# Per-head signals in the first block's attention, with the memory transposes and first scores moved into the last value chunk and the first memory-key chunk into the last steps

## The chip, the cores and the metric

The kernel runs on one core of one Trainium2 chip, in one launch. The metric is the device time of that launch in microseconds (us). The five engines of the core run their own instruction lists and meet only at semaphores: TensorE (PE in the rows, with PEld for its weight loads), VectorE (DVE), ScalarE (ACT), GpSimd (POOL) and SyncE (SP), which issues the weight loads.

## The reference, cut to what matters

Two transformer blocks on one sequence of 512 tokens, width 1024, all in float32.

- Block 1: RMS norm; a projection into eight heads of "forgetting" attention (head width 64, causal, each logit with a decay c_t - c_s from a cumulative sum of log gates) and eight heads of chunked attention with a relative bias; each head group normed; an output projection; residual. Then cross attention to 256 memory rows (four heads of width 256; the memory has its own RMS norm and a key/value projection `w_mem_kv`), residual; then SwiGLU of hidden width 2816, residual.
- Block 2: RMS norm; a projection of 4608 columns for three groups of dilated-window attention, whose queries and keys are normed per head; output projection, residual; RMS norm and a SwiGLU with a depthwise convolution of three taps; residual.

## The kernel before, in words

**Matmuls.** Float32 products are made from three matmuls on split operands (high part by high part, high by low, low by high; helper `three`, lines 1797 to 1799). Activations lie transposed in `a_hi` and `a_lo` (eight tiles of 128 features by 512 tokens). Weights come as chunks of 128 x 2048 (1 MB): SP loads a chunk into one of two `raw` slots, ACT copies it to `w_hi` (line 800), DVE, or POOL for some chunks (`pool_splits`), subtracts to get `w_lo` (line 1233, POOL 727), PE uses it. A slot is written again when the chunk that used it is done (`tile_done`), so the split of chunk c+1 runs beside PE's chunk c. All loops over chunks are in the order of the list `GEMMS`: forget, fox_qk, fox_v, chunk_qk, chunk_v, mem_k, mem_v, mix_out, mem_q, and so on. Each engine's order is written out by hand; nothing is planned by a tool.

**Around the attention of block 1.** PE ends `chunk_v` (two chunks of 48 matmuls; the second has four blocks b of 128 tokens, 12 matmuls each). Then it transposes the normed memory rows (16 transposes of 128 x 128, `turn`, line 2022, banks 4 to 7; ACT writes `a_hi`, line 1017, DVE `a_lo`, line 1551), then makes the scores of pairs 0 and 1 of heads, and begins the steps.

**The steps.** 32 pairs of heads (`HeadPair`): two heads by one block of 128 queries, i = b % 4 saying how many key blocks there are (i + 1). Pairs 0 to 15 have decays, pairs 16 to 31 a bias. At step t:

- PE: transposes of the probabilities of pair t (`pair_turned`, line 2161); scores of pair t + 2 (`pair_scores`, lines 2143, 2147, 2150); values of pair t (`pair_values`, through `by_column_group`, line 2048).
- DVE: `pair_out(t-1)` (line 1579), the reciprocal of the row sums and the copy of head 0's transposes to SBUF (`first_out`, lines 1588, 1591), the maxima of pair t + 2 (line 1563 with decays, 1570 with bias, where the biased scores are also written to `work`).
- ACT: the copy of head 1's transposes (`second_out`, line 1040), the two exponentials of pair t + 2 (`pair_exps`, lines 1029 and 1032).

One semaphore increment stands for both heads of a pair: `max_done`, `probs_done`, `turned`. The values of head 0 go to bank 2 and those of head 1 to bank 3, for every pair; so the values of pair t wait for `heads_done` of pair t - 1. After the last pair PE waits for all `heads_done` and begins `mem_k`: four chunks, each of two tiles of 24 matmuls with 256 columns.

**Three more places that the change touches.** (a) At `fox_qk` DVE works off the chain of the forget gates (lines 1491 to 1507), with the split of chunk 2 inside it, and only then evicts the tiles of chunk 0 (line 1520), whose banks chunk 2 of `fox_qk` writes. (b) Before `dil_in`: `residual` scales and adds eight tiles of the residual (POOL adds tiles 2 to 7, line 722) and writes `a_lo` (line 1281); `invert_pre("mixer_2")` then sums the eight squares in one reduction (line 1260); PE turns the sums to token order (`by_token`, line 1985), `invert_mixer` makes a diagonal (line 1271) and PE spreads it (`spread`, line 2014). (c) After `dil_out`: DVE adds its eight tiles to the residual (line 1741) and PE's `conv_up` waits (`enter`) until all eight are out of their banks; ACT splits the second chunk of `conv_up` before it makes `a_hi` of tiles 4 to 7, POOL subtracts for it (line 727), DVE writes `a_lo` (line 1281) and then sums the squares (line 1260).

## Time and profile before

| | |
|---|---|
| median of 3 runs | 1558.02 us (1558.0 to 1559.74) |
| the profiled execution's own time | 1563.09 us |
| its span in the profile | 1561.3 us |
| mean granted TensorE clock | 0.991 |
| PE busy | 1515.5 us, 97% of the span |
| PEld, DVE, ACT, POOL busy | 1235.7, 850.1, 602.0, 240.3 us |

The span is what the profile covers; the time of the execution lies 1.8 us above it. A busy time is the union of an engine's instructions; the ends of matmuls are modelled, so a PE shown busy may still be a PE at half clock, and the clock has its own column (1.00 is 2.4 GHz, 0.50 is 1.2 GHz). What PE waited for is in the view of waits; where in time, in the view by stretches and in the timeline.

### The profile page before, as it was taken

The page shows a single profiled execution, that of the slowest core. Times are in us where ns is not written, and L with a number is a line of the kernel's source. Part 1 is how long each engine was busy: PE and PEld are TensorE (multiplying, and loading weights), DVE is VectorE, ACT ScalarE, POOL GpSimd, SP SyncE. Part 2 cuts the span into 40 slices and gives each one's busy share as a digit, 9 for nine tenths or more (in the row PEclk, how much of TensorE's full clock was granted, in tenths as well). Part 3 has the DMA queues.
Part 4 walks back from the last instruction along what each step waited for, and adds up shares of the span by engine and source line. Part 5 has one row for each costly group of instructions (what it writes and reads, how often), then busy time and mean ns, then how long its engine had stood idle before and what let it go on. Part 6 is the DMA issues. An engine that isn't in the chain of part 4 may idle for free.

```text
span 1561.3 us, 21409 instructions
## 1 busy us (share of the span) xinstructions
PE 1515.5 (97%) x7988; PEld 1235.7 (79%) x7988; DVE 850.1 (54%) x1104; ACT 602.0 (39%) x923; POOL 240.3 (15%) x266
## 2 busy tenths in 40 slices
PE   9999988999998999999999899999999999999998
PEld 6787667887887888888888588888887788888887
DVE  6433564527545543433323786756876776767323
ACT  6222554643244322222323543335764433333222
POOL 0200000024014100000000554554542000000000
PEclk9999899999999999999999999999999999999999
DMA  5532002431112223333232123222002333232321
GB/s 166 190 97 92 1 2 64 153 108 54 55 55 81 81 81 107 93 96 108 81 107 90 50 77 108 81 98 91 2 1 82 96 91 107 81 107 82 109 105 54
DMA packets 152809, 132.22 MB, mean 85 GB/s; under 512 B 6300, under 2 KB 137628, under 8 KB 152740
## 3 DMA queue, kind: packets, MB, share of 16 engines
q1 hardware_dynamic: 150836, 128.11, 26.5%
q0 software_dynamic: 848, 3.17, 0.6%
q8 instruction: 46, 0.75, 0.2%
q14 instruction: 23, 0.19, 0.0%
q10 hardware_dynamic: 1056, 0.00, 0.0%
HBM read 129.15 MB, written 2.12 MB: 84 GB/s over the span
## 4 chain that ended last, share of the span: by engine, by line
PE 85%; DVE 5%; POOL 3%; ACT 3%; issue 3%; DMA 0%; ACTq 0%; SPq 0%; DVEq 0%; POOLq 0%
PE ps L1797 25%; PE ps L1798 25%; PE ps L1799 25%; PE ps L2048 2%; POOL other_stats L774 2%; PE ps L2161 1%; POOL x_t L722 1%; PE ps L2143 1%; PE ps L459 1%; PE ps L2058 1%; DVE a_lo L1281 1%; PE ps L1985 1%; ACT work L914 1%; PE ps L2014 0%; ACT w_hi L800 0%
## 5 line engine op out<-in xcount | busy, mean ns | idle before, releaser
L1797 PE MATMUL ps<-a_hi,w_hi 128*128 128x512 f32 (+2 forms) x1656 | 645.4, 390 | 14.8 <-DVE a_lo L1281 5.7
L1799 PE MATMUL ps<-a_hi,w_lo 128*128 128x512 f32 (+2 forms) x1656 | 639.9, 386 | 0.0
L1798 PE MATMUL ps<-a_lo,w_hi 128*128 128x512 f32 (+2 forms) x1656 | 639.8, 386 | 0.0
L1797 PEld LDWEIGHTS ps<-a_hi,w_hi 128*128 128x128 f32 (+1 forms) x1656 | 311.3, 188 | 87.9 <-issue 10.2
L1799 PEld LDWEIGHTS ps<-a_hi,w_lo 128*128 128x128 f32 (+1 forms) x1656 | 311.5, 188 | 64.0
L1798 PEld LDWEIGHTS ps<-a_lo,w_hi 128*128 128x128 f32 (+1 forms) x1656 | 311.6, 188 | 62.1 <-issue 0.7
L800 ACT ACTIVATE w_hi<-raw 128x2048 fp32r<-128x2048 f32 x118 | 225.8, 1913 | 348.5 <-PE ps L1799 346.4
L1233 DVE TENSOR_TENSOR w_lo<-raw,w_hi 128x2048 fp32r<-128x2048 f32 x94 | 215.3, 2290 | 245.0 <-ACT w_hi L800 244.7
L727 POOL TENSOR_TENSOR w_lo<-raw,w_hi 128x2048 fp32r<-128x2048 f32 x24 | 110.6, 4609 | 452.9 <-ACT w_hi L800 452.9
L1654 DVE TENSOR_TENSOR arena<-ps,rstd 128x512 f32<-128x512 f32 x88 | 60.2, 689 | 166.3 <-PE ps L1799 159.9
L1724 DVE RECIPROCAL rstd<-std 128x512 f32<-128x512 f32 x24 | 80.5, 3353 | 26.3 <-ACT std L1147 26.3
L1210 ACT ACTIVATE arena<-arena,vec 128x512 f32<-128x512 f32 x44 | 35.5, 815 | 110.3 <-DVE arena L1654 110.3
L1797 PE MATMUL ps<-w_hi,a_hi 128*128 128x512 f32 x192 | 74.9, 390 | 0.1
L1799 PE MATMUL ps<-w_hi,a_lo 128*128 128x512 f32 x192 | 74.9, 390 | 0.0
L1798 PE MATMUL ps<-w_lo,a_hi 128*128 128x512 f32 x192 | 74.9, 390 | 0.0
L2048 PEld LDWEIGHTS ps<-arena,work 128*64 128x64 f32 x1120 | 38.7, 138 | 27.2 <-issue 16.7
L2048 PE MATMUL ps<-arena,work 128*64 128x64 f32 x1120 | 47.1, 228 | 12.3 <-DVE work L1591 4.3
L1087 ACT ACTIVATE arena<-arena 128x512 f32<-128x512 f32 x22 | 13.9, 632 | 89.4 <-DVE arena L1654 89.4
L1775 DVE SCALAR_TENSOR_TENSOR arena<-arena,vec 128x384 f32<-128x384 f32 x88 | 48.0, 546 | 0.0
L1772 DVE SCALAR_TENSOR_TENSOR arena<-arena,vec 128x127 f32<-128x127 f32 x88 | 36.6, 416 | 12.6 <-DVE arena L1654 5.6
L1797 PEld LDWEIGHTS ps<-w_hi,a_hi 128*128 128x128 f32 x192 | 36.0, 188 | 8.1 <-DVE w_lo L1233 0.5
L1799 PEld LDWEIGHTS ps<-w_hi,a_lo 128*128 128x128 f32 x192 | 36.0, 188 | 7.6
(242 smaller groups left out, 1459.3 us busy)
## 6 DMA issues: line engine op xcount, KB each, us to landing
raw<-in_w_gate_up SPq DMA_DIRECT2D x44, 512.0 KB, 4.6
raw<-in_ffn_w_up SPq DMA_DIRECT2D x44, 512.0 KB, 4.6
raw<-in_attn_w_in SPq DMA_DIRECT2D x36, 512.0 KB, 4.4
raw<-in_w_in SPq DMA_DIRECT2D x24, 512.0 KB, 4.7
raw<-in_w_down SPq DMA_DIRECT2D x22, 512.0 KB, 4.0
raw<-in_ffn_w_down SPq DMA_DIRECT2D x22, 512.0 KB, 4.0
raw<-in_w_mem_kv SPq DMA_DIRECT2D x16, 512.0 KB, 4.2
raw<-in_w_out SPq DMA_DIRECT2D x8, 512.0 KB, 3.9
```

The lines of the kernel that those rows point to most:

```text
L727: pool.tensor_tensor(w_lo[:, ch.next_slot, :], raw[:, ch.next_slot, :], w_hi[:, ch.next_slot, :].bitcast(F), ALU.subtract).then_inc(weight ...
L800: act.activation(w_hi[:, ch.next_slot, :], raw[:, ch.next_slot, :], ACT.Copy).then_inc(weights_hi, 1)
L1210: act.activation(conv[:, 2 * ch.slot_o + j, :], up[:, 2 * ch.slot_o + j, :], ACT.Identity, bias=vcol("conv_b", ch.c + j * FT), scale=vcol( ...
L1233: dve.tensor_tensor(w_lo[:, ch.next_slot, :], raw[:, ch.next_slot, :], w_hi[:, ch.next_slot, :].bitcast(F), ALU.subtract).then_inc(weights ...
L1654: dve.tensor_tensor(up[:, 2 * ch.slot_o + j, :], ps[:, 2 * ch.slot_o + j, :], rstd[:, :], ALU.mult).then_inc(signal, 1)
L1724: dve.reciprocal(rstd[:, :], std[:, :]).then_inc(dil_rstd, 1)
L1772: dve.scalar_tensor_tensor(out=residues(u)[:, 0:tap, 1:128], in0=residues(src)[:, 4 - tap:4, 0:127], scalar=scalar, in1=residues(u)[:, 0:t ...
L1775: dve.scalar_tensor_tensor(out=u[:, tap * 128:S], in0=src[:, 0:S - tap * 128], scalar=scalar, in1=u[:, tap * 128:S], op0=ALU.mult, op1=ALU ...
L1797: pe.matmul(dst, s_hi, m_hi, start=start, stop=False, skip_group_check=across)
L1798: pe.matmul(dst, s_hi, m_lo, start=False, stop=False, skip_group_check=across)
L1799: return pe.matmul(dst, s_lo, m_hi, start=False, stop=stop, skip_group_check=across)
L2048: last = pe.matmul(dst[c, :], stationary[:, c], moving, start=start, stop=stop, skip_group_check=True)
```

## The change

1. **Signals by head.** New semaphores `pair_max`, `pair_probs` and `second_turned`: maxima, exponentials and transposes of a pair signal head by head, and what waits for them waits by head. With decays the one reduction over both heads becomes two. ACT's order at a step is: exponential of pair t + 1, head 0; copy of head 1's transposes of pair t; exponential of pair t + 1, head 1. DVE's is: maxima of t + 1, `pair_out(t-1)`, copy of head 0's transposes, reciprocal. The values of a pair lie in one bank (2 + b % 2), and wait for `heads_done` of pair t - 2.
2. **Inside the last value chunk.** PE's second `chunk_v` chunk has the 16 memory transposes after its block 0, the scores of pairs 0 and 1 after its block 2, then block 3. ACT's and DVE's lists are reordered to match, and ACT loads the table of the exponential earlier.
3. **First key chunk.** The two tiles of the first `mem_k` chunk take the place of the missing scores at steps 30 and 31 (banks 4 and 5); the second chunk writes banks 6 and 7, and only then PE waits for all `heads_done`. POOL makes both halves of the split of the second `mem_k` chunk during the attention.
4. **fox_qk.** The tiles of chunk 0 are evicted ahead of DVE's split of chunk 2.
5. **mixer_2.** Four squares are reduced, POOL adds tiles 4+5 and 6+7 in place, and DVE adds the two sums; the spread is four matmuls of a broadcast column by the identity, without the diagonal. POOL's `memset` of `q_pad_2` moves into `dil_in`.
6. **ffn_2.** DVE reduces the first four squares between tiles 4 and 5 of `dil_out`; ACT makes `a_hi` 4 and 5, the split, `a_hi` 6 and 7, then the squares; POOL's subtraction waits for `a_lo` of tile 7; `conv_up` no longer waits for the last `dil_out` tiles as a whole, only for its own two banks.

```diff
 def pool_splits(ch):
-        ch.gemm.name in ("mem_q", "ffn_up", "conv_up") and (ch.first_of_gemm or ch.second_of_gemm))
+        ch.gemm.name in ("mem_q", "ffn_up", "conv_up") and (ch.first_of_gemm or ch.second_of_gemm)) or (
+        ch.gemm.name == "mem_k" and ch.first_of_gemm)
...
+            def both_halves(ch):
+                pool.wait_ge(raw_loaded[ch.next_slot], ch.next_loads)
+                pool.wait_ge(tile_done, ch.before)
+                pool.tensor_copy(w_hi[:, ch.next_slot, :], raw[:, ch.next_slot, :]).then_inc(weights_hi, 1)
+                split_lo(ch)
+            both_halves(Chunk(G["mem_k"], 0, 2, 0))
...
             add_residual("ffn_post", y_ffn)
-            pool.memset(q_pad_2, 0.0).then_inc(pad_2_cleared, 1)
+            for k in (4, 6):
+                pool.wait_ge(norms["mixer_2"].sq, k + 2)
+                pool.tensor_tensor(y_ffn[:, k, :], y_ffn[:, k, :], y_ffn[:, k + 1, :], ALU.add)\
+                    .then_inc(norms["mixer_2"].value, 1)
...
+            pool.wait_ge(norms["ffn_2"].ready, KT)
             for c in range(2):
                 split_lo(Chunk(G["conv_up"], 0, 2, c))
...
+            act.wait_ge(tile_done, v_chunks[1].before)
+            for f in range(4):
+                mem_hi(f)
+            chunk_values(0)
+            for f in range(4, KT):
+                mem_hi(f)
...
+            for half in range(2):
+                pair_exp(PAIRS[0], half)
+            chunk_values(1)
             for t in PAIRS:
+                if t.b + 1 < BLOCKS:
+                    pair_exp(PAIRS[t.b + 1], 0)
                 second_out(t)
-                if t.b + 2 < BLOCKS:
-                    pair_exps(PAIRS[t.b + 2])
+                if t.b + 1 < BLOCKS:
+                    pair_exp(PAIRS[t.b + 1], 1)
...
             over_chunks(act, G["dil_out"], wide, peel=1)
+            act.wait_ge(tile_done, G["dil_out"].signal_end)
+            only_hi("ffn_2", x_block2, (4, 5))
             split_hi(Chunk(G["conv_up"], 0, 2, 0))
-            gained_hi("ffn_2", x_block2, range(4, KT))
+            only_hi("ffn_2", x_block2, (6, 7))
+            for k in range(4, KT):
+                squared("ffn_2", k)
...
             dve.reciprocal(w, u_).then_inc(gate_step, 1)
+            for j in range(2):
+                query_key(Chunk(G["fox_qk"], 0, 2, 0), j, 0)
             split_lo(Chunk(G["fox_qk"], 0, 2, 1))
...
+            pair_maxima(PAIRS[0])
             for t in PAIRS:
+                if t.b + 1 < BLOCKS:
+                    pair_maxima(PAIRS[t.b + 1])
                 if t.b:
                     pair_out(PAIRS[t.b - 1])
                 first_out(t)
-                if t.b + 2 < BLOCKS:
-                    pair_maxima(PAIRS[t.b + 2])
+                pair_recip(t)
...
+                    if ch.c == 1 and j == 0:
+                        half_sum("ffn_2")
...
             def pair_turned(t):
-                pe.wait_ge(probs_done, CREDIT + t.b + 1)
                 for half in range(2):
+                    pe.wait_ge(pair_probs, 2 * t.b + half + 1)
                     for a in range(t.i + 1):
                         last = pe.transpose(t.turned[:, half, cols], t.probs[:, half, cols], ident[:, :])
-                last.then_inc(turned, 1)
+                    last.then_inc(second_turned if half else turned, 1)
             def pair_values(t):
-                pe.wait_ge(turned_read, CREDIT + t.b + 1)
-                pe.wait_ge(second_read, t.b + 1)
-                pe.wait_ge(heads_done, CREDIT + t.b)
+                if t.b >= 2:
+                    pe.wait_ge(heads_done, CREDIT + t.b - 1)
                 for half in range(2):
+                    if half == 0:
+                        pe.wait_ge(turned_read, CREDIT + t.b + 1)
+                    else:
+                        pe.wait_ge(second_read, t.b + 1)
...
+            token_chunk(v_chunks[1], 4, range(4), None,
+                        lambda b: mem_transposed() if b == 0 else first_scores() if b == 2 else None)
+            first_keys = Chunk(G["mem_k"], 0, 2, 0)
             for t in PAIRS:
                 pair_turned(t)
                 if t.b + 2 < BLOCKS:
                     pair_scores(PAIRS[t.b + 2])
+                elif t.b + 2 == BLOCKS:
+                    chunk_ready(first_keys)
+                    feature_tile(first_keys, 0, 4, N_MEM)
+                else:
+                    feature_tile(first_keys, 1, 5, N_MEM)
                 pair_values(t)
-            pe.wait_ge(heads_done, CREDIT + BLOCKS)
-            feature_major("mem_k", "chunk_v", N_MEM)
+            feature_major("mem_k", "", N_MEM, peel=1)
...
+            def spread_mixer(norm):
+                pe.wait_ge(norm.inverse, 1)
+                for b in range(4):
+                    last = pe.matmul(ps[:, 5, b * 128:(b + 1) * 128], tok_eps_mean[:, b:b + 1].to_broadcast([128, 128]),
+                                     ident[:, :], start=True, stop=True, skip_group_check=True)
+                last.then_inc(norm.spread, 1)
...
-            feature_major("conv_up", "dil_out", ready=norms["ffn_2"].ready, tail=1)
+            feature_major("conv_up", "", ready=norms["ffn_2"].ready, tail=1)
```

## Rows read from the trace of the kernel before

**Rows 1.** The page: busy time of PE, and the chain that ended last.
```profile
PE 1515.5 (97%) x7988; PEld 1235.7 (79%) x7988; DVE 850.1 (54%) x1104; ACT 602.0 (39%) x923; POOL 240.3 (15%) x266
...
PE 85%; DVE 5%; POOL 3%; ACT 3%; issue 3%; DMA 0%; ACTq 0%; SPq 0%; DVEq 0%; POOLq 0%
```
**Rows 2.** Waits of PE, whole span: waited for, total us, times, longest.
```profile
PE ps L2048 <- DVE work L1591: 4.3, 7, 1.1
PE ps L2048 <- ACT work L1040: 3.8, 4, 1.0
PE ps L2048 <- issue: 3.8, 4, 1.3
...
PE ps L1797 <- DVE arena L1520: 1.9, 1, 1.9
...
PE ps L2014 <- DVE work L1271: 1.5, 1, 1.5
...
PE ps L1985 <- DVE work L1260: 1.3, 1, 1.3
...
PE ps L1797 <- DVEq L1743: 0.8, 1, 0.8
```
**Rows 3.** By stretches: length, busy time of each engine, granted clock, DMA.
```profile
153.00:160.00 7.00, 5.19 (x33) 3.49 (x32) 3.65 (x9) 6.40 (x15) 0.00 (x0) 0.86 0.00 0
160.00:175.15 15.15, 14.39 (x133) 9.68 (x132) 6.82 (x16) 6.07 (x21) 0.00 (x0) 0.73 0.00 1
175.15:186.90 11.75, 10.87 (x136) 7.91 (x132) 6.35 (x16) 5.82 (x21) 0.00 (x0) 1.00 0.01 1
210.15:220.82 10.67, 8.87 (x118) 6.02 (x116) 6.79 (x28) 6.17 (x21) 0.00 (x0) 1.00 0.01 2
242.20:253.69 11.49, 7.89 (x111) 5.42 (x109) 5.99 (x22) 6.94 (x17) 1.45 (x4) 1.00 0.01 2
253.69:276.75 23.06, 23.06 (x192) 23.06 (x193) 8.98 (x4) 8.21 (x10) 0.00 (x0) 1.00 0.42 137
181.04:181.97 0.93, 0.92 (x9) 0.71 (x8) 0.66 (x3) 0.93 (x3) 0.00 (x0) 1.00 0.00 0
184.71:185.82 1.11, 1.11 (x9) 0.79 (x8) 0.69 (x1) 0.60 (x1) 0.00 (x0) 1.00 0.00 0
```
**Rows 4.** Timeline of PE at 152.8: start, length, first half of the transposes.
```profile
152.78 1.03 PE L2022 MATMUL ps<-ident,arena 128*128 128x128 f32 x8
```
**Rows 5.** Timeline, a step with decays: ACT's copy, PE's values.
```profile
182.25 0.49 ACT L1040 ACTIVATE work<-ps 128x384 f32<-128x384 f32 x1
...
182.84 0.92 PE L2048 MATMUL ps<-arena,work 128*64 128x64 f32 x24 [0.87 <-issue]
```
**Rows 6.** Timeline, a biased step: maximum, exponential, copy; PE's transposes, values.
```profile
213.68 0.69 DVE L1570 CUSTOM_DVE_ANT_0 work<-ps,arena 128x512 f32<-128x512 f32 x1 [0.38 <-PE ps L2143]
...
215.02 0.72 ACT L1032 ACTIVATE work<-work,neg_max 128x512 f32<-128x512 f32 x1 [0.71 <-DVE neg_max L1570]
...
215.03 0.88 PE L2161 MATMUL ps<-ident,work 128*128 128x128 f32 x6
...
216.45 0.47 ACT L1040 ACTIVATE work<-ps 128x384 f32<-128x384 f32 x1
...
217.02 0.92 PE L2048 MATMUL ps<-arena,work 128*64 128x64 f32 x24 [0.70 <-DVE work L1591]
```
**Rows 7.** Before `dil_in`: line 1281 (min/median/max ns), the reduction, POOL's additions.
```profile
L1281 DVE SCALAR_TENSOR_TENSOR a_lo<-x_t,vec,a_hi x8: 750/1181/2271, 870.1 to 883.7; 128x512 fp32r<-128x512 f32 x8
...
L1260 DVE TENSOR_REDUCE work<-arena 128x512 f32<-128x4096 f32 x1 | 7.5, 7530 | 0.0
...
873.14 9.79 POOL L722 TENSOR_TENSOR x_t<-x_t,arena 128x512 f32<-128x512 f32 x6 [1.30 <-DVE arena L1293]
```
**Rows 8.** After `dil_out`: DVE's additions of tiles 4 to 6; POOL's subtractions (the page).
```profile
1184.58 2.35 DVE L1741 TENSOR_TENSOR x_t<-x_t,ps 128x512 f32<-128x512 f32 x3
...
L727 POOL TENSOR_TENSOR w_lo<-raw,w_hi 128x2048 fp32r<-128x2048 f32 x24 | 110.6, 4609 | 452.9 <-ACT w_hi L800 452.9
```

More of the change, by code:

```diff
@@ L799, in split_hi @@
                     act.wait_ge(tile_done, ch.before)
+                if ch.gemm.name == "mem_k" and ch.second_of_gemm:
+                    act.wait_ge(weights_split, ch.g + (1 + CREDIT))
                 act.activation(w_hi[:, ch.next_slot, :], raw[:, ch.next_slot, :], ACT.Copy).then_inc(weights_hi, 1)
@@ L1034, in pair_exps @@
-                last.then_inc(probs_done, 1)
+                at = slice(t.slot + half, t.slot + half + 1)
+                if t.decays:
+                    act.activation(t.probs[:, half, :], t.scores[:, half, :], ACT.Exp, bias=neg_max[:, at],
+                                   accum_out=row_sum[:, at]).then_inc(pair_probs, 1)
+                else:
+                    act.activation(t.probs[:, half, :], t.probs[:, half, :], ACT.Exp, scale=-1.0, bias=neg_max[:, at],
+                                   accum_out=row_sum[:, at]).then_inc(pair_probs, 1)
@@ L1229, in split_lo @@
                     return
-                if ch.gemm.name in ("mem_q", "ffn_up", "dil_out", "conv_up"):
+                if ch.gemm.name in ("mem_k", "mem_q", "ffn_up", "dil_out", "conv_up"):
                     dve.wait_ge(weights_split, ch.g + (1 + CREDIT))
@@ L1822, in feature_chunk @@
                     cols = slice(j * 128, j * 128 + 128)
+                    bank = 6 + j if ch.second_of_gemm and ch.gemm.name == "mem_k" else (bank0 + j) % 4
                     for k in range(k_tiles):
-                        last = three(ps[:, (bank0 + j) % 4, 0:tokens], (whi[:, k, cols], wlo[:, k, cols]),
+                        last = three(ps[:, bank, 0:tokens], (whi[:, k, cols], wlo[:, k, cols]),
                                      (a_hi[:, first + k, 0:tokens], a_lo[:, first + k, 0:tokens]), k == 0, k == k_tiles - 1)
@@ L1839, in _, with feature_tile @@
             post_norm = {"mix_out": "mix_post", "mem_o": "mem_post"}
+            def feature_tile(ch, j, bank, tokens):
+                whi, wlo = weights(ch.slot, KT)
+                pe.wait_ge(freed[ch.gemm.freed_by], ch.freed + (j + 1))
+                cols = slice(j * 128, j * 128 + 128)
+                for k in range(KT):
+                    last = three(ps[:, bank, 0:tokens], (whi[:, k, cols], wlo[:, k, cols]),
+                                 (a_hi[:, k, 0:tokens], a_lo[:, k, 0:tokens]), k == 0, k == KT - 1)
+                last.then_inc(tile_done, 1)
             def closing(ch):
@@ L1913, in body @@
                         closing(ch)
+                    elif name == "mem_k" and ch.first_of_gemm:
+                        return
+                    elif name == "mem_k" and ch.second_of_gemm:
+                        feature_chunk(ch, 2, tokens)
+                        pe.wait_ge(heads_done, CREDIT + BLOCKS)
                     else:
```

213 lines of the change are left out of this document (133 added, 80 removed).

## The prediction, made blind

> **What bounds the kernel now.** I read the page first: PE is busy 97% of the span and carries 85% of the chain that ended last [rows 1]. So time can come only from PE's own idle time, from stretches where its clock is down, or from work taken off it. The change takes almost no matmul away. The second view is therefore PE's waits over the whole span [rows 2]. The largest by far stand at line 2048, the values of the attention steps: 4.3 + 3.8 + 3.8 = 11.9 us in 15 waits. Three more belong to places that the change edits: 1.9 us at `fox_qk`, 1.3 + 1.5 us before `dil_in`, 0.8 us at the start of `conv_up`. The third view is by stretches, cut where the first transposes of every fourth pair start [rows 3]. A group of four pairs with decays lasts 11.75 us with PE busy 10.87; a biased group 10.67 with 8.87; the last group, to the start of `mem_k`, 11.49 with 7.89. The first group lasts 15.15 us although its work is that of the next, and its granted clock is 0.73: part of it ran at 1.2 GHz. Before it lies a stretch of 7.00 us in which PE did only the memory transposes and two scores, busy 5.19. The fall follows that thin stretch; the later groups have idle time too, and the clock stays at 1.00.
>
> **The change part by part.** All is measured against the profiled execution: span 1561.3, own time 1563.09, which lies 5.1 us (0.3%) above the median of the runs, 1558.02. I take the saving off the median.
>
> 1. *fox_qk.* The two evictions of chunk 0 now come before DVE's split of chunk 2. They need a tile long finished. PE's one wait of 1.9 us [rows 2] goes; what is late next is that split, two evictions (some 1.3 us by an eviction's length) later than now, while PE still has half a chunk to run. The end of the gate chain moves by the same amount, but then has two evictions fewer to do, so DVE is level again at the split of chunk 3. Bounds 1.0 and 1.9; I take **1.9**.
>
> 2. *From the end of the value chunks to pair 0.* Now 152.78 to 160.0, 7.2 us [rows 3, 4]. What is left of it as PE work, inserted between value blocks: 16 transposes, 2 x 1.03 = 2.1 at most [rows 4]; scores of pair 0, 0.93, and of pair 1, 1.11, taken from pairs 4 and 5, which have the same shape [rows 3]. The ACT and DVE copies of the transposes are covered by value blocks 1 and 2 (the rest of the chunk); the scores come just as they end, for which I add 0.1. Sum 4.2, saving **3.0**. If the cover fails, up to 1 us of it returns.
>
> 3. *Group one.* It should run like a steady group: 10.87 of work instead of 15.15 [rows 3], plus one new wait: ACT now must copy out value blocks 2 and 3 before the exponential of pair 1, and behind those stands head 1's copy of pair 0, for which PE's values wait. I estimate 0.4 (between 0 and 1). 11.3 instead of 15.15: **3.9**. This assumes the clock is not lowered, as no thin stretch is left.
>
> 4. *Decay groups two to four.* Each has one long wait, before the values of the third pair: 0.87 [rows 5], the last 1.3 (the waits named "issue", 3.8 in 4 times, one of them in group one). It is ACT's copy of head 1, at 182.25, behind two exponentials of the four-block pair; PE starts 0.1 after it ends. In the new order only one exponential stands ahead of the copy, and that can start when head 0's maximum is out. The copy comes about one exponential (0.7) and half a reduction (0.5) earlier, more than the wait. Total waits 3.8 less group one's 0.8 = 3.0; I leave 0.1 per group: **2.7**. Against it stands one more reduction per pair on DVE, busy 6.35 of 11.75 [rows 3], which covers it.
>
> 5. *Biased groups.* Idle 1.8 of 10.67. Follow the third pair [rows 6]. The maxima of the four-block pair start at 213.68, some 0.2 after its scores end, and are out at 215.0; exponentials 215.02 to 216.45, copy to 216.92, values at 217.02: 3.5 after the scores. By the new order, counted from the end of those scores: maximum of head 0 out at 0.85 (0.69 of work), its exponential (0.72 and the read of the sum) at 1.7, the copy (0.47) at 2.2, values at 2.3. PE meanwhile does the values of the second pair (two thirds of 0.92, 0.6), the transposes of the third (0.88, of which 0.8 before the next can start) and one-block scores, which I put at 0.45: it is done at 1.85. So a wait of about 0.45 stays, and the other three go, among them those on `heads_done`, now two pairs back. 8.8 + 0.45 = 9.25 instead of 10.67, 1.4 for each of three groups: **4.3**. Bounds 0.8 and 1.8 a group.
>
> 6. *Last group.* Without the scores of two further pairs the steps wait longest: 11.49 - 7.89 = 3.6 idle [rows 3]. Two tiles of `mem_k` go in, each 24 x 0.12 = 2.88 of full work (192 matmuls in 23.06) [rows 3], which has to be done anyway; after step 31 the second chunk follows without waiting for the last `heads_done`. All **3.6** go. POOL splits for the second chunk early in the attention, where it has nothing else to do; the third chunk's split by ACT and DVE begins at the end of tile 1 and has values 31 and a chunk of 5.8 us over it.
>
> 7. *mixer_2.* Waits 1.3 + 1.5 = 2.8 [rows 2]. The reduction over eight squares, 7.5 us, becomes one over four (3.8) and two additions of 0.7, 2.3 us shorter, so the first wait goes; the diagonal's work on DVE goes, and so the second. Against: four matmul pairs for one, some 0.4; and POOL's new additions begin at 882.9, when its sixth is over (873.14 + 9.79), just as DVE has `a_lo` of tiles 6 and 7 left. Line 1281 takes between 0.75 and 2.27 us [rows 7], the longer ones where POOL reads SBUF, so the last `a_lo`, and with it PE's opening chunk, can be some 1.1 later. Between 1.3 and 2.4; I take **1.7**, nearer to the late end.
>
>    The Trainium skill says the same as a rule ("SBUF — State Buffer", Who interferes with whom): a VectorE instruction with two SBUF inputs and a GpSimd instruction that reads SBUF hold a port against each other for a whole instruction. By it alone the tile is 1.1 late for certain and this part would bring 1.3. The spread of row 1281 agrees with it.
>
> 8. *ffn_2.* The 0.8 before `conv_up` [rows 2] turns into a like one: the half reduction (3.8 us) is put between tiles 4 and 5 of the residual, at about 1185.3, after the first of the three additions of [rows 8]; tile 5 leaves bank 1 at about 1190 instead of 1186, when `conv_up` has just begun and wants that bank. What goes is the hold of `a_lo` 4 to 7 by POOL's subtraction, 4.6 us long [rows 8], which now comes after them; of that hold PE felt perhaps 1 us. On the other side POOL is then done with the second chunk, 4.6 after `a_lo` 7, at about the moment when PE asks for it. Between -0.5 and 1.8; I take **1.0**.
>
> Sum: 1.9 + 3.0 + 3.9 + 2.7 + 4.3 + 3.6 + 1.7 + 1.0 = 22.1. 1558.0 - 22.1 = **1535.9, so 1536 us**.
>
> **The rivals.**
>
> *The clock falls anyway.* Group one, or another stretch nearby, is still granted 1.2 GHz for about as long as now. For it: transposes and scores with 64 rows now sit among the value blocks, and the steps are made of such matmuls. Against: steady groups with 0.9 to 1.8 us idle held 1.00. It costs 15.15 - 11.75 = 3.4: 1539.5.
>
> *The waits only change their name.* ACT's new order puts head 1's exponential behind the copy, so transposes of head 1 wait where values waited. For it: in biased groups the chain scores, maximum, exponential, copy is still longer than PE's own 1.85. Against: the transposes that would wait are due 0.9 later than the values. If parts 4 and 5 bring a fifth of what I count, 5.6 are lost: 1541.5.
>
> *Slower: the steps are held at 1.2 GHz throughout.* Its place is the 32 steps. Group one did 14.39 of busy time at 0.73, which is 10.5 at full clock; at 0.5 a group would take 21 instead of 11.3, so each group at half clock costs 9 to 10 us. It decides from the point where more than two of the eight groups run so (22.1 / 9.7 = 2.3); with three, 1558 + 7 = 1565. Against it speak six steady groups at 1.00 with more idle than they will have.
>
> *The edits around dil_in and conv_up bring nothing* (port and late weights), all else as forecast: 1538.7.
>
> **How the numbers follow.** The forecast 68%, clock 10%, names 10%, dil_in and conv_up nothing 8%, slower 2%, and 2% that the attention edits do not take effect in time at all. Range: gains of 15 to 28 us; the low end is all upper bounds of parts 5, 7 and 8 with parts 2 and 3 whole, 1530, the high end the second rival with a little more, **1530 to 1543**. What a measurement here can tell from no change is about 0.2%, 3 us; faster than that 95%, within it 3%, slower 2%.
>
> **What would show it right or wrong.** In the profile after: no wait of 1.9 at `fox_qk`; PE without a gap between the value chunk and pair 0, and a granted clock of 1.00 from 150 to 250; decay groups of 10.9 to 11.1 us and biased ones of 9.2 to 9.4, with one wait left each, before the third pair's values; `mem_k` matmuls between steps 30 and 31; the reduction of line 1260 at 3.8 us and no wait at the spread. Wrong it would be if the waits at line 2048 came back at the transposes of head 1, if a low clock moved to another place, or if the start of `dil_in` or the second `conv_up` chunk is held by POOL for more than 1.5 us.

## The result, and the profile after

The changed kernel took **1535.4 us** (median of 4 runs, 1534.7 to 1535.85) against 1558.01 (1557.78 to 1559.74) for the kernel before beside it: a ratio of 0.9851, 95% interval 0.9835 to 0.9866. The forecast was 1536, in a range of 1530 to 1543. In later runs on other chips the changed kernel took 1536.5, and the kernel before 1560.2 to 1560.6; beside each other on one chip they were 1536.5 and 1560.3, 23.8 us apart. Why the kernel before has two medians is told below. One run of one experiment took 1874 us at a mean granted clock of 0.75; it was disturbed and is left out.

The page of the profile after: engines with their busy time, and the chain that ended last. They answer to [rows 1]. PE is busy 8 us less, while the span is 28 us shorter: most of what went is waiting. Part of the 8 is not less work but more of it at full clock.

```profile
span 1533.2 us, 21458 instructions
...
PE 1507.1 (98%) x7994; PEld 1231.6 (80%) x7994; DVE 839.4 (55%) x1121; ACT 600.6 (39%) x923; POOL 248.0 (16%) x270
...
PE 91%; DVE 4%; POOL 2%; ACT 1%; issue 1%; DMA 1%; SPq 0%; ACTq 0%; DVEq 0%; POOLq 0%
```

PE's waits over the whole span, against [rows 2]: waited for, total, times, longest. Of 11.9 us at the values of the steps (now line 2173) 1.8 are left; the 1.9 of `fox_qk` and the 1.3 and 1.5 before `dil_in` are gone; the 0.8 at `conv_up` stands, under a new line.

```profile
PE ps L1897 <- DVE a_lo L1363: 4.6, 4, 2.5
PE ps L2388 <- DVE arena L1480: 2.4, 1, 2.4
PE ps L2220 <- POOL arena L680: 2.4, 1, 2.4
PE ps L2173 <- DVE work L1679: 1.8, 4, 0.5
...
PE ps L1897 <- DVEq L1841: 0.8, 1, 0.8
```

Stretches of four pairs, against [rows 3]. T(0) is the start of the first transposes of pair 0, and group one begins there. The rows are groups one, two and five, and the last group up to the start of its second `mem_k` tile. Columns: length, busy time and count of each engine, granted clock, DMA share, GB/s.

```profile
154.72:165.72 11.00, 10.89 (x134) 7.88 (x132) 6.31 (x19) 7.61 (x24) 6.42 (x2) 1.00 0.27 83
165.72:176.44 10.72, 10.72 (x136) 7.85 (x133) 6.50 (x20) 6.06 (x21) 0.00 (x0) 1.00 0.04 15
197.34:206.59 9.25, 8.74 (x120) 6.01 (x116) 6.49 (x28) 6.18 (x21) 0.00 (x0) 1.00 0.01 2
225.09:234.34 9.25, 9.25 (x105) 7.27 (x101) 4.73 (x19) 4.52 (x15) 0.00 (x0) 1.00 0.01 3
```

A third biased pair in the timeline after, against [rows 6], DVE, ACT and PE in this order. Both maxima come first (210.13 and 210.75), then the output of the pair before, and only then the copy of head 0 at 211.56, which ends at 212.11. ACT's copy of head 1 ends at 212.06. PE's values start at 212.26, after a wait of 0.51, the only one that this group has left.

```profile
210.13 0.69 DVE L1663 CUSTOM_DVE_ANT_0 work<-ps,arena 128x512 f32<-128x512 f32 x1 [0.38 <-PE ps L2261]
210.75 0.69 DVE L1663 CUSTOM_DVE_ANT_0 work<-ps,arena 128x512 f32<-128x512 f32 x1
211.36 0.28 DVE L1671 TENSOR_TENSOR arena<-ps,row_recip 128x128 f32<-128x128 f32 x1
211.56 0.55 DVE L1679 COPY work<-ps 128x384 f32<-128x384 f32 x1
...
210.87 0.72 ACT L1092 ACTIVATE work<-work,neg_max 128x512 f32<-128x512 f32 x1 [0.59 <-DVE neg_max L1663]
211.59 0.47 ACT L1099 ACTIVATE work<-ps 128x384 f32<-128x384 f32 x1
211.96 0.71 ACT L1092 ACTIVATE work<-work,neg_max 128x512 f32<-128x512 f32 x1
...
211.25 0.49 PE L2261 MATMUL ps<-arena 64*128 64x128 f32 x4
212.26 0.92 PE L2173 MATMUL ps<-arena,work 128*64 128x64 f32 x24 [0.51 <-DVE work L1679]
```

### The profile page after: what moved, and what is told of

Its sections match the earlier page's. It is cut to its first block, busy times and chain, and to the rows that moved or that the text cites. A ratio compares the mean times of both kernels' runs of the same rounds, so it can differ in the third digit from the quotient of the medians.

```text
span 1533.2 us, 21458 instructions
## 1 busy us (share of the span) xinstructions
PE 1507.1 (98%) x7994; PEld 1231.6 (80%) x7994; DVE 839.4 (55%) x1121; ACT 600.6 (39%) x923; POOL 248.0 (16%) x270
## 4 chain that ended last, share of the span: by engine, by line
PE 91%; DVE 4%; POOL 2%; ACT 1%; issue 1%; DMA 1%; SPq 0%; ACTq 0%; DVEq 0%; POOLq 0%
PE ps L1897 26%; PE ps L1899 25%; PE ps L1898 25%; PE ps L2173 2%; POOL x_t L746 2%; PE ps L2261 1%; PE ps L2279 1%; DVE work L1343 1%; PE ps L465 1%; PE ps L2183 1%; PE ps L567 1%; PE ps L2364 1%; PE ps L2101 1%; DVE a_lo L1363 1%; DMA arena<-in_x 1%
## 5 line engine op out<-in xcount | busy, mean ns | idle before, releaser
L709 POOL TENSOR_TENSOR w_lo<-raw,w_hi 128x2048 fp32r<-128x2048 f32 x25 | 115.2, 4607 | 447.6 <-ACT w_hi L828 416.3
```

The lines of the kernel that those rows point to most:

```text
L709: pool.tensor_tensor(w_lo[:, ch.next_slot, :], raw[:, ch.next_slot, :], w_hi[:, ch.next_slot, :].bitcast(F), ALU.subtract).then_inc(weight ...
```

## The experiments

Each is told as a small edit of the changed kernel, except the two further profiles of the kernel before. Its median can be set beside 1536.5, that of the first experiment. Medians of one kernel moved by about 1 us between chips (1535.4 and 1536.5 for the changed one), so effects under 1.5 us are read in the profile, at their place. Low-clock stretches elsewhere in the kernel also come and go: from the first head mean to the token sums of `ffn_2` the changed kernel took 306.7 us in one profile (granted clock 1.00) and 308.3 in the other (0.99).

### The changed kernel again

> The changed kernel once more, as the yardstick of the other runs of this chip. Expected 1535.4 us (1534.7 to 1536), and a profile with a granted clock of 1.00 from 150 to 250 us. If the saving of the first profile (28.1 us between the two spans, against 22.6 between the medians) came from a lucky choice of low-clock stretches after the change, this span would be longer than 1533.2 by some us; if it came from an unlucky profile of the kernel before, this span stays within 1 us of 1533.2.

Measured: 1536.48 us (1535.8 to 1536.81), span 1534.0, groups of 11.00, 10.72 and 9.25 us at clock 1.00. The saving of the first profile was no luck of the profile after. So the 5.5 us by which the two spans differ more than the medians lie in the profile of the kernel before.

### The transposes and scores back behind the chunk

```
+                pool.wait_ge(weights_split, ch.g + (1 + CREDIT))          # POOL, in both_halves
...
-            token_chunk(v_chunks[1], 4, range(4), None,
-                        lambda b: mem_transposed() if b == 0 else first_scores() if b == 2 else None)
+            token_chunk(v_chunks[1], 4, range(4), None)
+            mem_transposed()
+            first_scores()
```

(The first line is in this kernel and in the next: POOL's conversion for `mem_k` waits for the split before it.)

> Only the memory transposes and the first scores go back behind the last value chunk, all else as after the change. My theory: the thin stretch of some 7 us comes back, which costs the 3.0 us of part 2, and the clock falls behind it as before, which costs the 3.4 to 3.9 of part 3: 1541.8 to 1542.3 us, granted clock of the first group near 0.73. Rival: the fall of the clock had another cause (the order of the steps); then only the 3.0 come back, 1538.4, and the first group runs at 1.00.

Measured: 1543.3 us (1540.25 to 1543.35), 6.8 above the changed kernel: the sum of both prices, and the rival (3.0) is out. PE's one wait there is 3.6 us long, for `a_lo`; the stretches show the clock: it is at 1.2 GHz for part of the gap and part of group one (the granted clock is 0.50 from 155.8 to 165.9 us), and the group takes 13.79 us. One of the five runs took only 1540.25 us, at a mean granted clock of 0.995 against 0.991 to 0.993 of the others.

```profile
PE ps L2262 <- DVE a_lo L1643: 3.6, 1, 3.6
```
```profile
152.20:159.12 6.92, 3.33 (x17) 2.58 (x17) 3.78 (x10) 5.00 (x15) 4.82 (x2) 0.76 0.10 19
159.12:172.91 13.79, 13.79 (x133) 9.31 (x134) 7.06 (x21) 7.20 (x24) 0.00 (x0) 0.75 0.19 68
172.91:183.63 10.72, 10.72 (x136) 7.85 (x132) 6.50 (x20) 6.06 (x21) 0.00 (x0) 1.00 0.01 2
```

### The same gap, filled with matmuls

```
-            act.wait_ge(tile_done, v_chunks[1].before)
-            for f in range(4):
-                mem_hi(f)
             chunk_values(0)
-            for f in range(4, KT):
+            for f in range(KT):
                 mem_hi(f)
...
             mem_transposed()                     # as in the experiment before, and then
+            pe.wait_ge(freed["act"], CREDIT + G["chunk_v"].freed_end - 3)
+            for _ in range(14):
+                pe.matmul(ps[:, 0, :], decay[:, 0:128], decay, start=True, stop=True, skip_group_check=True)
             first_scores()
```

> The second experiment once more (memory transposes and first scores behind the last value chunk), but PE does 14 matmuls of 128x512 whose result nobody reads while it waits between transposes and scores, into the bank of value block 0, which ACT copies out first. There PE idled 3.59 us, the clock was at 1.2 GHz from 155.8 us on for 10 us, and the kernel took 1543.3 us. My theory (the fall follows the idle stretch): the clock stays at 1.00, T(0) near 157.5, the first group takes 11.0 to 11.4 us, 1539 to 1540 in all, and the 3 us of the gap stay lost. Rival: the fall belongs to this place of the kernel (its load by then) or to chance; group one again takes 13.8 us and more in the profile and the median lies at 1542 to 1543.5.

Measured: 1539.12 us (1538.97 to 1539.22). The line 2318 in the timeline is the filling. The stretches, to be held against those of the experiment before: busy throughout, clock 1.00, group one 10.90.

```profile
150.76 1.91 PE L2299 MATMUL ps<-ident,arena 128*128 128x128 f32 x16
152.42 3.43 PE L2318 MATMUL ps<-masks 128*128 128x512 f32 x14
155.79 0.49 PE L2259 MATMUL ps<-arena 64*128 64x128 f32 x4
```
```profile
152.20:157.75 5.55, 5.55 (x35) 4.28 (x34) 3.71 (x10) 3.48 (x11) 5.33 (x2) 1.00 0.00 0
157.75:168.65 10.90, 10.90 (x134) 7.93 (x133) 6.97 (x21) 7.73 (x26) 0.00 (x0) 1.00 0.31 98
```

With fourteen matmuls whose result nobody reads the time is 4.2 us shorter (1543.3 to 1539.1), and no fall is seen. The theory holds: the place of the kernel is as before, only the idle stretch is gone. Between these two kernels two things differ, the filling and ACT's earlier copies of two value blocks. The copies were not run apart, but they can hardly be the cause of the clock: T(0) moved by 1.37 us only (159.12 to 157.75), while group one lost 2.89; the two together are the whole difference of the spans (4.3). The 3 us of the gap itself stay: T(0) is at 157.75 against 154.4 to 154.9 in the changed kernel and the experiments that leave this stretch alone. Taken together, the fall near T(0) came in three of four profiles with the thin stretch (two of three of the kernel before, and the experiment before this one) and in none of the ten without it.

### The kernel before, twice more

> The kernel before the change once more with a profile of its own, since the first profile of it (span 1561.3) lay 5 us above the median of its runs. Expected: the low clock of some 10 us behind the memory transposes is there again (it belongs to the kernel), T(0) at 160 and a first group of 15.2 us as in [rows 3]; the low-clock stretches near 350, 500 and 1165 us are fewer or shorter than in the first profile (17 us in three places), and the span is 1556 to 1558. Rival: all of them are as before and the time is again near 1562; then the median of 1558 hides two kinds of run, and the difference between 28.1 and 22.6 us is not the clock's.

Measured: span 1558.9, own time 1560.7. T(0) stands at 159.83 again, but the fall behind it is not there: group one took 11.75 us. The times of low clock lie near 354, 494, 869, 893 and 1163 us. From the first head mean to the token sums of `ffn_2` this profile took 311.7 us, against 310.3 in the first.

```profile
159.83:171.58 11.75, 10.87 (x133) 7.91 (x133) 6.52 (x16) 6.08 (x21) 0.00 (x0) 1.00 0.01 1
171.58:183.32 11.74, 10.86 (x136) 7.91 (x133) 6.34 (x16) 5.82 (x21) 0.00 (x0) 1.00 0.00 1
```

My expectation failed: the fall does not belong to every run of this kernel.

> A third profile of the kernel before. In the first the clock was low for 10 us from T(0) on (group one 15.2 us), in the second not at all there (group one 11.75 us, median 1560.6 on the same chips). If the fall comes and goes, the third is one or the other and nothing between: 15.2 us with a span near 1560, or 11.75 us with 1556 to 1559; a value between would mean that it moves against the work.

Measured: span 1555.7, own time 1557.45. Group one took 12.55 us, between the two pure cases.

```profile
159.84:172.39 12.55, 11.67 (x133) 8.31 (x134) 6.72 (x16) 6.06 (x21) 0.00 (x0) 0.93 0.01 1
172.39:184.14 11.75, 10.87 (x137) 7.92 (x133) 6.35 (x16) 5.82 (x21) 0.00 (x0) 1.00 0.01 1
```

So in three profiles the fall cost group one 3.4, 0 and 0.8 us, with T(0) at the same place each time. My expectation said that a value between would mean a fall that moves against the work. It does not move: the granted clock is 0.50 from 158.3 to 161.6 us in the first profile and in the third, some 2 us before T(0) already. In the third it is 1.00 from 161.8 on, in the first it stays at 0.50 until 168.2, and in the second it is 1.00 throughout. What varies is whether the fall comes and how long it lasts. (The Trainium skill, "TensorE: Matmul & The Clock Gate", Part 1, says that the point at which the clock rises after the start of a kernel varies between runs of one kernel. These three profiles show a variation of another place, a fall inside the kernel, with 3.4 us between the ends.)

The runs of the kernel before differ in the same way. Of its 55 timed runs on the later chips 21 had a mean granted clock of 0.995 or 0.996, with a median of 1558.2 us; 34 had 0.990 to 0.993, with a median of 1561.6. The times of the two sets touch (1557.5 to 1560.2 and 1560.0 to 1564.3), and the lower clock is not always this fall: the second profile has 0.993 without it. Its span is still 3.2 us over that of the third: it took 3.0 us more from the first head mean to the token sums of `ffn_2` (311.7 against 308.7) and 0.9 more just before, and 0.8 less in group one. By its time the median of 1558.0 from which I took the saving belongs to the first set; the profile that I read, 1563.1, to the second. The changed kernel's runs spread by 2.1 us, from 1534.7 to 1536.8.

### ACT's order undone, signals kept

```
                 if t.b + 1 < BLOCKS:
                     pair_exp(PAIRS[t.b + 1], 0)
-                second_out(t)
-                if t.b + 1 < BLOCKS:
                     pair_exp(PAIRS[t.b + 1], 1)
+                second_out(t)
```

> In the steps ACT does both exponentials of the next pair before it copies head 1, the signals by head are kept. My theory: the signals by head carry most of parts 4 and 5 (7.0 us by the forecast); the order adds 0.25 to 0.7 us in each of the four biased groups, where the third pair's values would wait for the copy behind the second exponential, and nothing in the decay groups: 1536.4 to 1538.2, biased groups of 9.5 to 9.9 us instead of 9.25. Rival: ACT's order is what brought the saving; then 5 us or more come back, 1540.5, and the decay groups are longer too (11.2 and more).

Measured: 1537.9 us (three runs, 1537.09 to 1538.49), 1.4 above. A decay group takes 10.81 instead of 10.72, a biased one 9.45 instead of 9.25; group one 11.55 instead of 11.00, with one wait of 0.6 for ACT's copy, which I had not foreseen. The rival (5 us) is out.

```profile
166.17:176.98 10.81, 10.81 (x136) 7.93 (x132) 6.50 (x20) 6.01 (x22) 0.00 (x0) 1.00 0.01 2
198.13:207.58 9.45, 9.16 (x119) 6.16 (x117) 6.65 (x28) 6.07 (x21) 0.00 (x0) 1.00 0.01 2
```

### Orders kept, waits again for both heads

```
-                act.wait_ge(pair_max, 2 * t.b + half + 1)
+                act.wait_ge(pair_max, 2 * t.b + 2)
...
-                    pe.wait_ge(pair_probs, 2 * t.b + half + 1)
+                    pe.wait_ge(pair_probs, 2 * t.b + 2)
...
-                dve.wait_ge(turned, CREDIT + t.b + 1)          # first_out
+                dve.wait_ge(second_turned, t.b + 1)
...
-                    if half == 0:
-                        pe.wait_ge(turned_read, CREDIT + t.b + 1)
-                    else:
-                        pe.wait_ge(second_read, t.b + 1)
+                    pe.wait_ge(turned_read, CREDIT + t.b + 1)
+                    pe.wait_ge(second_read, t.b + 1)
```

> The counterpart of the order: ACT's and DVE's orders and single instructions by head are kept, but each wait is again for both heads (exponentials for both maxima, transposes for both exponentials, DVE's copy for both transposes, values for both copies). My theory: this alone undoes most of parts 4 and 5: decay groups of some 11.4 us and biased ones of 10.1, 5.6 us in all, 1541.0. Rival (order alone): no more than 1 us comes back, 1536.4. Worse than before the change it could be by 1 or 2 us in the decay groups, since two reductions cost DVE more than one.

Measured: 1540.64 us (1539.79 to 1541.51), 4.2 above; by the spans 5.7. The theory holds, the rival (no more than 1 us) is out. Groups of 11.18 and 10.07 us, and PE's waits of 154 to 232 us are back at the values:

```profile
166.39:177.57 11.18, 10.79 (x137) 7.88 (x133) 6.62 (x20) 5.93 (x21) 0.00 (x0) 1.00 0.01 2
199.75:209.82 10.07, 8.88 (x119) 6.05 (x117) 6.83 (x28) 6.19 (x21) 0.00 (x0) 1.00 0.01 2
```
```profile
PE ps L2173 <- ACT work L1099: 5.4, 11, 0.8
PE ps L2173 <- DVE work L1679: 0.8, 4, 0.2
```

The signals are worth about 0.5 in a decay group (11.18 against 10.72) and 0.8 in a biased one (10.07 against 9.25). From 11.75 and 10.68 before to 11.18 and 10.07 here it is the new orders, the shorter lookahead of the maxima, the two reductions by head and the wait for `heads_done` one pair further back; these were not taken apart.

### The evictions of fox_qk late again

```
-            for j in range(2):
-                query_key(Chunk(G["fox_qk"], 0, 2, 0), j, 0)
             split_lo(Chunk(G["fox_qk"], 0, 2, 1))
```

(and in `query_keys` the first chunk's tiles are evicted again.)

> At fox_qk alone DVE again splits chunk 2 before it does the two evictions of chunk 0, as before the change. My theory: PE's wait there comes back in full, +1.9 us, 1.9 above the changed kernel on the same chip (1537.3 to 1538.4). Rival: the lateness is taken up at the next wait; then +1.0 or less.

Measured: 1538.14 us (1536.53 to 1540.37), 1.7 above. PE's waits between 30 and 60 us have one row, where the changed kernel has none, and T(0) is at 156.79, 2.2 after the mean of its profiles. The wait is back in full, and nothing up to T(0) takes it up: the rival is out.

```profile
PE ps L1893 <- DVE arena L1570: 1.9, 1, 1.9
```

### The first mem_k chunk behind the steps again

```
-                elif t.b + 2 == BLOCKS:
-                    chunk_ready(first_keys)
-                    feature_tile(first_keys, 0, 4, N_MEM)
-                else:
-                    feature_tile(first_keys, 1, 5, N_MEM)
...
                 pair_values(t)
+            pe.wait_ge(heads_done, CREDIT + BLOCKS)
+            chunk_ready(first_keys)
+            feature_tile(first_keys, 0, 4, N_MEM)
+            feature_tile(first_keys, 1, 5, N_MEM)
```

> The two tiles of the first mem_k chunk go back behind the last step (and the wait for all heads with them), all else as after the change. My theory: the last group idles again for what is missing, +3.6 to 4.0 us: 1539.0 to 1540.5. Rival: with signals by head the last steps no longer wait long, so the tiles hide little and only 2 us come back: 1537.5 to 1538.

Measured: 1538.46 us (1537.98 to 1538.81), 2.0 above, and 2.0 in the profile too, from the start of the last group to the token sums of `mix_out`. The rival holds. The timeline of the last steps:

```profile
230.91 0.93 PE L2173 MATMUL ps<-arena,work 128*64 128x64 f32 x24 [0.94 <-DVE work L1679]
231.77 1.09 PE L2279 MATMUL ps<-ident,work 128*128 128x128 f32 x8
233.30 1.15 PE L2173 MATMUL ps<-arena,work 128*64 128x64 f32 x32 [0.44 <-DVE work L1679]
234.91 0.39 PE L1897 MATMUL ps<-a_hi,w_hi 128*128 128x256 f32 x1 [0.45 <-DVE arena L1671]
```

With the new signals and orders the last steps wait 0.94 + 0.44 + 0.45 = 1.83 us and not 3.6. The tiles hide these 1.8; the other half of the saving was there already.

### mixer_2 with one reduction

```
-                    half_sum(name)
-                    for k in (4, 6): ...                       # two additions
+                    dve.wait_ge(norm.sq, KT)
+                    dve.tensor_reduce(square_sum, of.rearrange("p k n -> p n k"), axis=AX.X, op=ALU.add)\
+                       .then_inc(norm.added, 3)
...
-            for k in (4, 6):                                   # POOL's pair additions
-                pool.tensor_tensor(y_ffn[:, k, :], y_ffn[:, k, :], y_ffn[:, k + 1, :], ALU.add)
```

> At mixer_2 DVE again sums all eight squares in one reduction (7.5 us) and POOL adds no pairs; that PE multiplies by the token means without a diagonal is kept. The first profile after the change showed 2.7 to 3.0 us saved there, where I had forecast 1.7. My theory: each of the two old waits was worth its whole length, and the port cost the opening chunk about a third of a us and not 1.1: the wait before the token sums comes back (1.3), the opening chunk ends 0.3 earlier, +1.0 us in all. Rival: the reduction carried nearly all; +2 us and more. Second rival: the pair additions cost as much as they bring; 0.

Measured: 1536.94 us (1535.58 to 1537.73), 0.5 above. At its place: from `ffn_post`'s token sums to those of `mixer_2` 28.85 us, as in the kernel before (28.87), against 27.69 and 27.74 in the changed kernel, so 1.1 to 1.2; from there to the first head mean 3.18 against 3.09, so the spread without diagonal keeps its gain. The timeline of DVE shows the last two `a_lo` and the reduction, of this kernel first and then of the changed one, with POOL's row of the pair additions:

```profile
859.41 1.46 DVE L1355 SCALAR_TENSOR_TENSOR a_lo<-x_t,vec,a_hi 128x512 fp32r<-128x512 f32 x1 [0.24 <-ACT a_hi L848]
861.11 0.75 DVE L1355 SCALAR_TENSOR_TENSOR a_lo<-x_t,vec,a_hi 128x512 fp32r<-128x512 f32 x1 [0.25 <-ACT a_hi L848]
861.78 7.54 DVE L1326 TENSOR_REDUCE work<-arena 128x512 f32<-128x4096 f32 x1
```
```profile
860.25 1.46 DVE L1363 SCALAR_TENSOR_TENSOR a_lo<-x_t,vec,a_hi 128x512 fp32r<-128x512 f32 x1 [0.24 <-ACT a_hi L853]
861.96 1.45 DVE L1363 SCALAR_TENSOR_TENSOR a_lo<-x_t,vec,a_hi 128x512 fp32r<-128x512 f32 x1 [0.24 <-ACT a_hi L853]
...
861.12 3.43 POOL L759 TENSOR_TENSOR arena<-arena 128x512 f32<-128x512 f32 x2
```

The pair additions cost the last `a_lo` 0.70 us (1.45 against 0.75), not 1.1, and the tile before takes 1.46 us beside POOL's residual in either kernel. The theory holds; the 0.3 that it expected back at the opening chunk can't be seen apart.

### POOL's split of conv_up no longer waits

```
-            pool.wait_ge(norms["ffn_2"].ready, KT)
```

> At ffn_2 POOL's splits again don't wait for the last a_lo; the half reduction and all else stays as after the change. My theory: the split runs beside the a_lo of tiles 4 to 7 and holds them for its 4.6 us; from the residual of dil_out to conv_up's second tile PE loses again about what the change brought, 0.8 to 1.1 us: 1537.3 to 1537.6. Rival: the moved squares brought it and the wait nothing; 0 within 0.3 us.

Measured: 1536.47 us (1535.31 to 1536.71), no difference that the median can tell. The profile tells one. Four `a_lo` in a row take 7.10 us with POOL's subtraction beside them and 2.80 without (this kernel first, then the changed one). Only one of the four is held: the third, begun 0.5 us after POOL's subtraction, takes 5.04 us, the others 0.74 to 0.75 as in the changed kernel. PE waits 0.4 us for them, and from the first head mean to the token sums of `ffn_2` this kernel takes 307.5 us against 306.7 in the first profile of the changed kernel, both at a granted clock of 1.00.

```profile
1165.81 5.00 POOL L709 TENSOR_TENSOR w_lo<-raw,w_hi 128x2048 fp32r<-128x2048 f32 x1 [29.11 <-ACT w_hi L827]
1164.91 7.10 DVE L1362 SCALAR_TENSOR_TENSOR a_lo<-x_t,vec,a_hi 128x512 fp32r<-128x512 f32 x4
```
```profile
1167.62 4.62 POOL L709 TENSOR_TENSOR w_lo<-raw,w_hi 128x2048 fp32r<-128x2048 f32 x1 [31.10 <-DVE a_lo L1363]
1164.74 2.80 DVE L1363 SCALAR_TENSOR_TENSOR a_lo<-x_t,vec,a_hi 128x512 fp32r<-128x512 f32 x4
```

The hold is real (4.3 us), and PE feels 0.8 of it. The median can't confirm the 0.8.

### A version that beats both

```
                 if t.b + 1 < BLOCKS:
-                    pair_maxima(PAIRS[t.b + 1])
+                    pair_maxima(PAIRS[t.b + 1], (0,))
+                first_out(t)
+                if t.b + 1 < BLOCKS:
+                    pair_maxima(PAIRS[t.b + 1], (1,))
                 if t.b:
                     pair_out(PAIRS[t.b - 1])
-                first_out(t)
...
-                    if ch.c == 1 and j == 0:
+                    if ch.c == 1 and j == 1:
                         half_sum("ffn_2")
```

> A version that might beat both kernels. In the steps DVE does the maximum of head 0 of the next pair, then copies head 0 of this pair, and only then does the maximum of head 1 and the output of the pair before: the copy was the last wait left (1.8 us in 4 times, behind both maxima). At ffn_2 the half reduction comes one residual addition later, so that conv_up's second bank is free when it begins. My theory: biased groups of 8.9 to 9.0 us instead of 9.25 (some 1.5 us in all with the first decay groups), and 0.8 us at conv_up: 2.3 below the changed kernel, 1534. Rival: ACT's exponential of head 1 then waits for the late maximum and passes the wait on to the transposes of head 1; steps as long as now or longer, only the 0.8 of ffn_2 stays, 1535.7.

Measured: **1533.5 us** (1531.89 to 1534.59), ratio to the kernel before 0.9826 (0.9813 to 0.984); 3.0 below the changed kernel's 1536.5 and 1.9 below its 1535.4; none of its five runs is as long as the shortest of the changed kernel's nine. The theory holds, the rival is out. Between 154 and 232 us PE has no wait at all, and none at `conv_up`; biased groups take 8.81 us, all of it busy, and DVE's copy of head 0 stands between the two maxima:

```profile
165.72:176.45 10.73, 10.73 (x137) 7.86 (x133) 6.49 (x20) 6.29 (x21) 0.00 (x0) 1.00 0.04 12
197.08:205.89 8.81, 8.81 (x121) 6.01 (x117) 6.63 (x28) 6.45 (x21) 0.00 (x0) 1.00 0.01 3
```
```profile
201.52 0.56 DVE L1679 COPY work<-ps 128x384 f32<-128x384 f32 x1 [0.20 <-PE ps L2281]
```

By place, the steps bring 1.6 us (0.3 in the decay groups, 1.3 in the biased ones), and the later half reduction 1.0 (307.3 us from the first head mean to the token sums of `ffn_2`, against 308.3 in the second profile of the changed kernel, both at a granted clock of 0.99).

## Why the prediction was right, and where it was not

The mechanism was right: waits of PE went at the places and, with the two exceptions told at parts 5 and 6, by the causes named. That the time came out within 0.6 us of the forecast is partly luck: errors of both signs cancelled, and the median of 1558.0 that the forecast started from was a low draw for the kernel before (1560.2 to 1560.6 later; the changed kernel was then 23.8 us below it and not 22.1). The first profile after (own time 1535.0) beside the third of the kernel before (1557.45), whose time is like that of the median. The places are the starts of the first transposes of every fourth pair, of the token sums, of the first head mean, and the end, as the timelines have them; the last 354.4 us are equal to 0.1.

| part | forecast | measured in these two profiles |
|---|---|---|
| 1 and 2, up to T(0) | 4.9 | 159.84 - 154.72 = 5.1 |
| 3, group one | 3.9 | 12.55 - 11.00 = 1.6 |
| 4, three decay groups | 2.7 | 34.98 - 31.62 = 3.4 |
| 5, three biased groups | 4.3 | 32.06 - 27.75 = 4.3 |
| 6, last group to mix_out | 3.6 | 103.89 - 99.89 = 4.0 |
| mix_out to ffn_post | 0 | 515.74 - 516.36 = -0.6 |
| 7, mixer_2 | 1.7 | 1.2 + 1.5 = 2.7 |
| 8 and the dilated part | 1.0 | 308.66 - 306.70 = 2.0 |
| sum | 22.1 | 22.5 |

- **Part 1.** Held: 1.9 in the waits, 2.2 at T(0).
- **Part 2.** Held: 3.0 forecast; with the gap filled, T(0) is 3.2 later than the mean of the changed kernel's two profiles.
- **Part 3.** The step that failed, by 2.3 us, is not the mechanism but its price. "It should run like a steady group", and then "11.3 instead of 15.15": it ran 11.0, at 1.00. But the 15.15 were those of one execution, and I took the whole difference off a median that such executions don't set. In the three profiles of before it would have been 4.2, 0.75 and 1.6. The rule that I wrote down, that the sum is made against the profiled execution, was not carried to its end: its own time lay 5.1 us over the median, and most of the 3.4 of the fall, which I counted as saved, belongs to that excess. The first profile of before is 5.6 us longer than the third, 2.65 of it in group one, 1.25 from mix_out to ffn_post and 1.65 from the first head mean to the token sums of `ffn_2`. The fall also began some 2 us before T(0), where I had it begin with group one.
- **Part 4.** Undersized by 0.7. I left 0.1 of wait per group; groups two and three have none (busy 10.72 of 10.72), and PE's own work is 0.15 shorter per group than the 10.87 before.
- **Part 5.** Right to the tenth, with the wait of about 0.45 where I put it (0.5). But its cause was half seen: I had it end with ACT's copy, while DVE's copy of head 0, behind two maxima and an output, is out at the same moment (212.11 and 212.06). The last experiment changed only DVE's order in the steps, and the wait was gone: ACT's copy, whose place in its list stayed, does not hold PE.
- **Part 6.** Right in size, wrong in the account. "All 3.6 go" was booked on the two tiles. The tiles bring 2.0 (measured with the new steps in place); the other 2.0 had gone by the new signals and orders together. With the tiles in place, undoing the signals alone costs this part only about 0.5 (100.4 us against 99.9): the two cover the same idle time.
- **Part 7.** Undersized by 1.0, above my upper bound of 2.4. I had the last `a_lo` 1.1 late and PE's opening chunk with it. It is 0.70 late, and the opening chunk ends 0.3 later after the token sums of `ffn_post` (23.77 us against 23.45 in the first profile of before). Both old waits were worth their full length.
- **Part 8.** 1.1 from the first eviction of `dil_out` to the token sums (30.1 us against 31.2); the hold of `a_lo` is 0.8 of it by experiment. The wait at `conv_up` came back as 0.8 where I said, behind the half reduction. Another 0.9 us I had not forecast: 0.3 lies between the first two head means, 0.5 in three steps of the dilated attention. No experiment shows the cause.

The row of the table from mix_out to ffn_post is the clock and not the change: the first profile after lies longer at low clock there (from 327.9 us on) than the second, which took 515.75 us, as the kernel before did. With that second profile the row is 0.0, and the one of part 8 is 308.66 - 308.31 = 0.35, since the low clock then lies there. The 2.0 of part 8 compares two stretches at 1.00; two at 0.99 (310.31 in the first profile of before, 308.31 in the second after) give the same.

The low end of the range does not follow from its own words: with the upper bounds of parts 5, 7 and 8 (5.4, 2.4 and 1.8) the sum is 24.7, which gives 1533, not the 28 us of 1530.

The Trainium skill's rule on the shared port ("SBUF — State Buffer", Who interferes with whom) is confirmed by the four `a_lo` of 2.80 and 7.10 us, one of which ended only after POOL's instruction had. In part 7 the price that I had worked out under it, 1.1 us, was too high: only one of the instructions met POOL's additions, it lost 0.70, and PE had other work.

**The rivals.** The clock fell nowhere between 150 and 250 us after the change, in two profiles of it and in those of the seven experiments that leave this stretch as it is. The waits did not change their name: transposes of head 1 never wait. The edits around `dil_in` and `conv_up` brought 3.8 us (2.7 and 1.1), the 0.9 without a known cause left out. The slower case was never near.

## What to carry to other kernels

Before a stretch of low clock is booked as a saving, profile the same kernel a second time: it may be in one execution and not in the next, and a term read from one profile belongs to the time of that profile, not to the median. Where a chain crosses three engines, signal for each piece that the next engine can use by itself, and then look for the engine whose list puts a later pair's work ahead of the copy that is waited for. When two edits cover the same idle time, undo each alone before either is credited with all of it.

## What the runs showed of the hardware

- With 14 matmuls of 128x512 without use, 3.43 us long, in a gap of PE the granted clock was 1.00 from 150 to 170 us; with the gap empty it was at 1.2 GHz in parts of the gap and of the 13.79 us behind it. The filled version was 4.2 us faster (ACT's order differed too).
- With T(0) at 159.83, 159.84 and 159.96 us in three executions of one kernel, the low-clock stretch around it was absent, short (group one 12.55 us) or long (15.15). In the two in which it came it had begun by 158.3 us. Over all kernels here it came in three of four profiles with the thin stretch before it and in none of the ten without.
- A subtraction of 128x2048 on POOL takes 4.62 us; running beside four `a_lo` on DVE it took 5.00 and made 7.10 us of their 2.80. One of the four took 5.04 instead of 0.75, the others were as before.
- POOL's conversion of 128x2048 (for the `mem_k` split, at 155.04 us in the changed kernel) took 1.88 us, about as long as ACT's 1.91 for the same work.
